# Stick-breaking attention: the short block's values computed right behind the long block's, and one output copy per cycle

## What is computed

```python
z = einsum('bqhd,bkhd->bhqk', q, k) * 64**-0.5 + bias
mask = k_pos[None, :] < q_pos[:, None]
log_keep = where(mask, log_sigmoid(-z), 0.0)
log_between = cumsum(log_keep, axis=3, reverse=True) - log_keep
a = where(mask, exp(log_sigmoid(z) + log_between), 0.0)
out = einsum('bhqk,bkhd->bqhd', a, v)
```

## Time and profile before

| what | value |
|---|---|
| time, median of 3 runs | 1183.25 us (1182.72 to 1184.02) |
| time of the profiled execution | 1181.27 us, span 1179.4 us |
| TensorE busy with matmuls | 1130.4 us (96%) |
| VectorE busy | 640.2 us (54%) |
| ScalarE busy | 338.6 us (29%) |
| GpSimd busy | 251.9 us (21%) |
| mean granted TensorE clock | 0.994 of full speed |
| prompt attention | from about 353 us to 572 us of the span |

### The profile page before, as it was taken

One profiled execution on the slowest core, in us unless ns is written; L12 is line 12 of the kernel. 1 busy time (PEld: TensorE's weight loads), 2 busy tenths in 40 slices (PEclk: granted clock), 3 DMA queues, 4 the chain that ended last, 5 costly groups with the idle time before them and its releaser, 6 DMA issues.

```text
span 1179.4 us, 19535 instructions
## 1 busy us (share of the span) xinstructions
PE 1130.4 (96%) x6692; PEld 540.2 (46%) x6692; DVE 640.2 (54%) x1273; ACT 338.6 (29%) x719; POOL 251.9 (21%) x303
## 2 busy tenths in 40 slices
PE   6999999999998989998999999999999999999996
PEld 3444444444445666666544444533333333333332
DVE  0010687877779999999985574832223223223222
ACT  2132221222118879898312222100100000000010
POOL 2011102220228910000010011113323322322322
PEclk9999999999999999999999999999999999999999
DMA  9942322223328465654523346699977798976993
GB/s 358 359 138 107 126 101 92 84 99 108 111 75 291 154 207 184 211 172 167 218 89 108 107 164 237 227 380 338 355 244 287 262 356 287 338 280 250 344 359 131
DMA packets 122486, 250.78 MB, mean 213 GB/s; under 512 B 15150, under 2 KB 29614, under 8 KB 121384
## 3 DMA queue, kind: packets, MB, share of 16 engines
q1 hardware_dynamic: 101729, 206.85, 49.6%
q0 software_dynamic: 16704, 38.30, 9.2%
q10 hardware_dynamic: 3984, 4.72, 1.2%
HBM read 370.93 MB, written 38.17 MB: 347 GB/s over the span
## 4 chain that ended last, share of the span: by engine, by line
PE 77%; DVE 13%; issue 5%; DMA 3%; ACT 2%; SPq 0%; POOL 0%; DVEq 0%; POOLq 0%; ACTq 0%
PE bank L2045 21%; PE bank L1635 21%; PE bank L2058 10%; PE bank L1826 7%; PE bank L1615 3%; DVE big L2331 3%; DVE big L2341 2%; DVE cvT L2382 2%; PE bank L2035 2%; PE bank L1490 1%; DMA h_d<-low 1%; DMA mid<-in_w_ada_dram 1%; PE bank L1697 1%; PE bank L1669 1%; PE bank L1942 1%
## 5 line engine op out<-in xcount | busy, mean ns | idle before, releaser
L2045 PE MATMUL bank<-big,mid 128*64 128x512 f32 x1104 | 250.9, 596 | 0.0
L1635 PE MATMUL bank<-big 128*128 128x512 f32 x560 | 244.5, 594 | 0.1
L1635 PEld LDWEIGHTS bank<-big 128*128 128x128 f32 x560 | 105.0, 190 | 128.0 <-issue 127.9
L2226 DVE SCALAR_TENSOR_TENSOR cvT<-low,cw,cvT 128x256 f32<-128x256 f32 x360 | 156.9, 510 | 0.0
L2045 PEld LDWEIGHTS bank<-big,mid 128*64 128x64 f32 x1104 | 77.9, 137 | 144.8 <-issue 144.8
L2058 PE MATMUL bank<-big,mid 128*64 128x512 f32 x544 | 119.6, 592 | 0.0
L2331 DVE TENSOR_TENSOR_SCAN big<-big 128x513 f32<-128x513 f32 (+4 forms) x96 | 91.0, 987 | 0.7 <-ACT big L1231 0.6
L2923 DVE TENSOR_TENSOR xt<-xt,bank 128x512 f32<-128x512 f32 x18 | 12.4, 688 | 124.7 <-ACT xt L1432 123.4
L915 POOL TENSOR_TENSOR st<-st,mhalf 128x16 f32<-128x16 f32 (+1 forms) x9 | 25.2, 2801 | 246.5 <-DVE st L2257 237.2
L2058 PEld LDWEIGHTS bank<-big,mid 128*64 128x64 f32 x544 | 39.1, 137 | 77.7 <-issue 77.7
L2941 DVE TENSOR_TENSOR mid<-bank,low 128x512 f32<-128x512 f32 x34 | 21.9, 686 | 95.9 <-PE bank L2058 95.9
(11 more groups left out here) (463 smaller groups left out, 1410.0 us busy)
## 6 DMA issues: line engine op xcount, KB each, us to landing
big<-in_w_gate_dram SPq DMA_DIRECT2D x74, 1024.0 KB
big<-in_w_up_dram SPq DMA_DIRECT2D x72, 1024.0 KB
big<-in_w_down_dram SPq DMA_DIRECT2D x72, 1024.0 KB
low<-in_w_ada_dram SPq DMA_DIRECT2D x32, 512.0 KB, 5.5
low<-in_cache_v_dram SPq DMA_DIRECT2D x64, 256.0 KB
big<-in_w_in_dram SPq DMA_DIRECT2D x8, 1280.0 KB, 17.1
xt<-in_x_prompt_dram SPq DMA_DIRECT2D x16, 512.0 KB, 5.7
mid<-in_w_ada_dram SPq DMA_DIRECT2D x8, 1024.0 KB, 14.0
```

What stands on the lines that cost most here:

```text
L1635: mm = pe.matmul(bank[:, 4 if cc == 2 else cc, :], hT[:, s, k, :], w_in_sb[:, k, cc * 512:(cc + 1) * 512], start=(k == 0), stop=(k == KD - 1))
L2045: mm = pe.matmul(bank[half, 2 * s + w, :], xgT[:, s, k, half], held[x][:, k, :], start=(k == 0), stop=(k == KD - 1))
L2226: c.put(V.scalar_tensor_tensor(out, src, cw[:, ch, tap:tap + 1], out, ALU.mult, ALU.add))
```

## The change

In a cycle the short unit's `values` move from behind `turn_a(3c)` to right behind the long unit's `values`, ahead of `scores(3c+2)`. The two units write two halves of bank 6: query blocks 4 to 7 columns 128 to 255, blocks 0 to 3 columns 0 to 127. Only the long unit waits for `o_sb`; the short one now follows without that wait, but it still waits for its own `at_sb`. ScalarE copies both outputs in one operation of 256 columns, in the place of the old evac_o(2c-2), and this now waits for both units; the copy behind keeps(3c+3) is gone. At the end of the attention both units' values stand ahead of the last strips_to_o.

```diff
-            def evac_o(u):
-                pair, qb = unit(u)
-                act.wait_ge(S["pv_mm"], u + 1)
-                nc.scalar.activation(oT[:, pair, qb * P:(qb + 1) * P], bank[:, 6, 0:P], ACT.Copy).then_inc(S["o_sb"], 1)
+            def evac_o(c):
+                pair, lo = unit(2 * c + 1)
+                hi = unit(2 * c)[1]
+                blocks = oT[:, pair, 0:SEQ].rearrange("p (b n) -> p b n", n=P)
+                act.wait_ge(S["pv_mm"], 2 * c + 2)
+                nc.scalar.activation(blocks[:, lo:hi + 1:hi - lo, :], bank[:, 6, 0:2 * P].rearrange("p (b n) -> p b n", n=P),
+                                     ACT.Copy).then_inc(S["o_sb"], 2)
@@ ScalarE, cycle
                 if c >= 1:
-                    evac_o(2 * c - 2)
+                    evac_o(c - 1)
                 keeps(3 * c + 2)
...
                     keeps(3 * c + 3)
-                if c >= 1:
-                    evac_o(2 * c - 1)
@@ ScalarE, end
             evac_aT(3 * CYCLES - 1)
-            evac_o(U - 2)
-            evac_o(U - 1)
+            evac_o(CYCLES - 1)
@@ TensorE, values(u)
-                if u >= 1:
+                if u % 2 == 0 and u >= 2:
                     pe.wait_ge(S["o_sb"], u)
+                half = 1 if qb >= NTP // 2 else 0
...
-                        mm = pe.matmul(bank[64 * h:64 * h + 64, 6, 0:P],
+                        mm = pe.matmul(bank[64 * h:64 * h + 64, 6, half * P:(half + 1) * P],
@@ TensorE, cycle
                     turn_a(3 * c - 1)
                     values(u - 2)
+                    values(u - 1)
                 scores(3 * c + 2)
...
                 turn_a(3 * c)
-                if c >= 1:
-                    values(u - 1)
@@ TensorE, end
             turn_a(3 * CYCLES - 1)
             values(U - 2)
+            values(U - 1)
             strips_to_o(DB - 1)
-            values(U - 1)
```

## The result

The changed kernel takes 1188.08 us (median of 7 runs, 1186.30 to 1189.76), the kernel before 1183.83 in the same comparison. The ratio is 1.0037 with a 95% interval of 1.0027 to 1.0047: slower by 4.25 us between the medians (4.4 by the ratio). 1188.2 was predicted.

The account below looks back on a forecast made before the run. VectorE was taken to set the pace, with 1.57 us idle in 150. Delays in cycles 2, 6, 7, 10, 11, 14 and 15 summed to 5.0 us, giving 1186.3 profiled and 1188.2 us as median; 8-in-10 range 1183.5 to 1191.0.

Parts of the forecast that it names:

- The price of the block: TensorE ahead of scores(3c+2): n moved matmuls delay them by 0.38, 0.59, 0.81 or 1.03 us for n of 4 to 16.
- The new wait: TensorE ahead of the short values: stands still for evac_aT(3c-1), 0.47 us in cycles 7 and 11, 0.44 in 9.
- The return: TensorE behind turn_a(3c): time freed there is nothing in cycles with c % 4 of 2 or 3, as pages wait for ScalarE.
- Most comes back: Cycles 8 and 12 (c % 4 = 0): TensorE itself is late, so most of the block's 1.03 us is regained.
- The lags: TensorE's delay carried between cycles: 0.59 - 0.2 us into cycle 7, 0.25 into cycle 10.
- the first rival: Slack takes the delay; only cycles 7 and 11 show, 1 to 2 us together; about 1184.8 us, chance 0.24.
- ScalarE's copy: ScalarE: one 256-column copy replaces two of 128, taking 0.403 us; the saving is hidden by VectorE and counted as nothing.
- The bound by full durations: ScalarE's saving from the merge at most: 0.21 us a cycle, 3.1 us over 15 cycles, if ScalarE were the bound.
- The 1.4 us by the page of the Trainium skill: ScalarE's saving by the skill's costs: one instruction fewer saves 93 ns a cycle, 1.4 us over 15.
- the sensitive instructions are the copies behind the scan of 3c+1: VectorE's copies L2362 and L2370 feel TensorE's delay, for example 1.6 us in cycle 7 and 0.7 in 10.
- the second rival: TensorE and ScalarE become the bound throughout, every unreturned delay counts: 9 us over 15 cycles, about 1192 us, chance 0.12.
- TensorE's own waits for VectorE: TensorE waits 4.8 us for VectorE, in cycles 4, 5 and 13, wiping out its lag: 0 for cycles 3-5, 12, 13.

Follow-up runs that it names:

- e8: Kernel before with only the new wait added: TensorE waits for evac_aT(3c-1) ahead of scores(3c+2), short values in their old place; ratio to before 1.0007.
- e12: Kernel before with as many extra, overwritten matmuls as the short unit has, issued ahead of scores(3c+2), old place kept; ratio to before 1.0042, stage +4.17 us.
- e4: Kernel before with the change made only in cycles 1, 4, 5, 8, 9, 12, 13 and at the attention's end; ratio to before 1.0011.
- e2: Kernel before with the merged copy alone, TensorE's order as before; 1183.58 us against 1182.42, ratio 1.0004.
- e5: Changed kernel with VectorE's copies L2362 and L2370 moved behind weigh(3c+1); ratio to before 1.0042, stage +3.94 us.
- e6: Kernel before with VectorE's copies L2362 and L2370 moved behind weigh(3c+1); 1183.56 us against 1182.30, ratio 1.0013.
- e11: Kernel before with the short unit's matmul group issued twice in the old place behind turn_a(3c); ratio to before 1.0042, stage +2.31 us.
- e1: Changed kernel with the move kept and the merged copy undone into two of 128 columns; 1188.09 us against 1182.42 before, ratio 1.0043.
- e7: Changed kernel with the short values put behind the first two pages and the merged copy behind sigs(3c+2); ratio to before 1.0018.
- e9: Kernel before with ln_mean put ahead of scores_s in cycle 14; 1182.50 us against 1183.51, ratio 0.9988.
- e10: Changed kernel with ln_mean put ahead of scores_s in cycle 14; ratio to before 1.0031.
- e3: Kernel before with the change made only in cycles 2, 3, 6, 7, 10, 11, 14, 15; ratio to before 1.0036.

## Why the prediction was right

The mechanism was right: moved matmuls ahead of the scores, little return, VectorE made to wait. That the time agrees to 0.1 us is in part luck: 5.0 us were predicted on a start of 1183.2, and 4.25 us were measured on 1183.83, so two errors of 0.6 to 0.75 us cancel. Most terms of the sum can be held against a wait of the trace after, less what stood there before. Cycle 2: 0.5 predicted, 0.69 - 0.25 = 0.44. Cycle 6: 0.2, no wait. Cycle 7: 1.6, 1.35. Cycle 9: 0, 0.45 at its first scan. Cycle 10: 0.7, 0.38. Cycle 11: 0.8, 0.79. Cycle 14: 0.6, 2.24 - 1.72 = 0.52. Cycle 15: 0.6, 0.30. The measured waits add up to 4.23 us, the stage grew by 4.35, and 5.0 was predicted: every term was at or above its wait, except cycle 9.

**The price of the block**, 0.16 + n x 0.054: for 12 matmuls 0.81 predicted and 0.81 measured (454.75 to 455.56).

**The new wait**: 0.47 predicted in cycles 7 and 11 and 0.44 in cycle 9; 0.36, 0.35 and 0.18 measured. In cycle 7 the 0.1 for the signal was twice what the start times show (0.05). Its whole effect, 0.24 us of the stage in e8, was rightly the small part.

**The return**: "nothing" in types 2 and 3. The page's wait of 0.98 against 0.21 shows it for cycle 7, and e12 leaves at most 0.7 us for the whole stage. By the prediction's prices the emptied places are 10.2 us (4 x 0.38, 4 x 0.59, 4 x 0.81, 3 x 1.03), and 7.3 us of that stand in the list again as longer waits of the pages for evac_aT (9.3 less 2.0). "Most comes back" in type 0 was too kind: cycle 9 starts with a wait of 0.45, which the sum had at nothing and which e4, where only types 0 and 1 are moved, has alone with 0.69.

**The lags**: the sum carried 0.4 us of lag into cycle 7 and 0.25 into cycle 10. Cycle 6 does not wait, and cycles 7 and 10 wait 0.25 and 0.32 less than predicted. Here the first rival had a point: some of the lag is caught up on the way. Elsewhere its claim, that only cycles 7 and 11 show, is refuted.

**ScalarE's copy**: 0.403 us was taken from evac_aT's row, and 0.40 is measured in cycle 7. Its worth was put at nothing and e2 shows nothing (-0.06 us of the stage). The bound by full durations, 3.1 us, is excluded. The 1.4 us by the page of the Trainium skill (ScalarE: Activation LUTs, What ACT_TABLE_LOAD costs) are not seen either: that page gives the saving on the engine, and the engine does not set the end here.

**What failed** is the sentence that "the sensitive instructions are the copies behind the scan of 3c+1". As a way of reading slack it gave the right places. As a cause it fell with e5: with the copies out of the way 1.1 us of waiting goes and the stage is 0.4 us shorter, not 3. Nearer, by the reading above, is a part of the second rival: in cycles 6 to 9 and 10 to 14 TensorE and ScalarE are as critical as VectorE, and what delays scores(3c+2) delays their round. They are not the bound throughout, as it said: 9 us were its price, and in cycles 3 to 5 and 12, 13 the lag is gone without a wait of VectorE. There TensorE's own waits for VectorE took it, as predicted: 1.51 us in cycle 5 became 0.95, and 1.13 in cycle 13 is gone. What stays open is the rest of what e6, e11 and e12 take in time beyond their stages: after the estimates above for the clock it is 0.5, 1.3 and 1.4 us.

## What to carry to other kernels

Merging two small operations is worth their saving only if their engine sets the end; the move that makes the merge possible has to be priced first, by what then stands behind the moved work and by whether the place that it leaves was a hole. Work with slack belongs in the place where its engine waits anyway: here behind turn_a(3c), where TensorE waited for ScalarE, taking the short values away gave little back, though a second group there cost 2.31 us (e11), for the hole is finite. And when several engines are above 90% busy, the instruction that waits may be only where the lateness comes out; a trial that moves it away tells symptom from cause.

## What was not expected of the hardware

In cycle 15 of the kernel after, 64 matmuls took 3.40 us where the kernel before needs 1.95 for the same. The mean granted clock from 560 to 580 us was 0.91 there and 1.00 before, so for a few microseconds the clock was at the lower of its two levels, 1.2 instead of 2.4 GHz. Ahead of it TensorE had waited 2.16 us for VectorE (TensorE's timeline, kernel after):

```profile
567.60 1.06 PE L1697 MATMUL bank<-identf,big 128*128 128x128 f32 x8 [2.16 <-DVE big L2341]
568.60 3.40 PE L1753 MATMUL bank<-low,big 128*32 128x128 f32 x64
```

It cost nothing: e1, with the same waits of VectorE and 1.96 us for these matmuls, has the same stage length to 0.01 us. Since e1's TensorE stood still for the same 2.16 us, that wait alone does not decide whether the clock falls.

Behind the attention the lower clock goes with a longer time. Cut into stretches of 20 us from L2439 on, that part has no stretch with a mean clock of 0.91 in the kernel before, e2, e6, e7, e9 and e10, and takes 603.7 to 605.3 us; one in e1, e3, e4, e5 and e8, with 605.8 to 606.6; two in the kernel after and e12, with 608.6 and 609.6; three in e11, with 612.5. One such place in TensorE's timeline, before and then after:

```profile
720.93 0.44 PE L1868 MATMUL bank<-identf,low 128*128 128x128 f32 x2 [1.30 <-DVE low L2520]
...
721.86 2.84 PE L1927 MATMUL bank<-big 128*128 128x512 f32 x6
```

```profile
724.99 0.44 PE L1868 MATMUL bank<-identf,low 128*128 128x128 f32 x2 [1.88 <-DVE low L2520]
...
725.91 4.53 PE L1927 MATMUL bank<-big 128*128 128x512 f32 x6
```

The same six matmuls take 1.69 us longer after a wait of 1.88 us than after one of 1.30; in e11 the wait there is 2.96 us. None of the edits touches this part, and why its waits differ between executions is not shown. It is the reason to compare the stage length here, or the medians of many executions, and not single spans.
